# Two pauses in the order of a gated recurrence beside a projection

## The chip, the cores and the metric

One Trainium2 chip, one of its cores. The metric is the device time of one execution in microseconds (us); the kernel before was run three times, with one more execution under the hardware profiler. Engines are named PE (TensorE), DVE (VectorE), ACT (ScalarE), POOL (GpSimd) and SP (SyncE, which here only issues transfers).

## The reference, cut to what matters

The whole program is two transformer layers followed by a third block with another mixer, all in float32, 512 positions, width 1024. The change touches the mixer of the third block alone. It projects the positions `hx` (512 x 1024) and, for some columns, a context `hc` (256 x 1024) with one weight matrix, runs a bidirectional gated recurrence over four heads of 128 (first the context, then the positions), and an attention of 8 heads over positions and context:

```python
px = jnp.split(hx @ w_in[l], IN_SPLIT_IDX, axis=-1)     # q k v | hq hi ff fb hg
pc = jnp.split(hc @ w_in[l], IN_SPLIT_IDX, axis=-1)
...
fg = lb_d + (1.0 - lb_d) * jax.nn.sigmoid(f)            # hgrn2_prep
return silu(q) * HG_HEAD_DIM**-0.5, 1.0 - fg, i, jnp.log(fg)
...
# gla_chunked: S_t = diag(f_t) S_{t-1} + k_t v_t^T, o_t = S_t^T q_t
...
o = rmsnorm(o_f + flip(o_b), gain) * jax.nn.silu(g)     # readout
...
x = x + mx[2] * (jnp.concatenate([att_x, hg_x], axis=-1) @ w_out[l])
```

## The kernel before, in words

**Products.** Every projection streams its weights from memory in chunks of 128 output columns. ACT copies a chunk to a rounded half `w_hi` (`split_high`, line 160), DVE subtracts it to get the rest `w_lo` (`split_low`, line 166), two chunks ahead of their use, and PE makes three matmuls for each 128 rows of the weight (line 196): hi times hi, hi times low, low times hi. The accumulator banks 0 and 1 take turns.

**The second mixer** (`SecondMixer`, from line 1930) has 26 chunks, in the order of `SB_LIST`: the query of heads 0 and 1, then for each head its two gates `ff`, `fb`, (for heads 2 and 3 also `hq`) and its values `i`, and last k, v, four q and four `hg`. A chunk is cut into **parts** of 12 matmuls: two wide ones (512 positions) and, for the gates, values, k and v, two more on the context (256 positions), into bank 2. The 24 chunks behind the first pair make 76 parts, numbered p = 0 to 75. Parts 24 to 37 are head 2's: ff, fb (wide, wide, context, context each), hq (wide, wide), i (wide, wide, context, context); parts 38 to 51 are head 3's in the same way; 52 to 59 are k and v, 60 to 75 q and hg, wide only.

**The recurrence** is cut into 56 **jobs**: a head has two directions (a unit u is one of them), a unit has seven levels. One job n is a chain over four engines: DVE takes two differences of cumulated logs (lines 2295, 2296), ACT their exp (line 2162), POOL two multiplies (lines 2061, 2062), PE the level product (line 2452), and DVE puts the masked result into the weights (`select`, line 2318). Round these lie steps of a unit or a head at fixed job numbers (`due(n, first, every, number)`): on PE turning values (line 2462; n = 0 and 1 of each 14) and decayed keys (line 2469; n = 2 and 3, 9 and 10), the sums (lines 2479, 2482), the output (lines 2501, 2504; n = 18, 32, 46, 60) and its mean (line 2509; n = 20, 34, 48, 62); on ACT the copies of what PE turned (`v_out`, line 2132, n = 4 and 5 of each 14; `kd_out`, line 2124, n = 6 and 7 of each 7), `prepare` (lines 2111 to 2115, n = 1 of each 7), the output's square and copy (lines 2145, 2146; n = 22, 36, 50, 64), its ln and exp (lines 2152, 2154; n = 24, 38, 52, 66); on DVE the four scans of a head (lines 2282, 2284; `SCANS`, before the difference of n = 13, 27, 41), the states (lines 2303 to 2309, n = 3 of each 7, from 10), the gain (line 2336; n = 26, 40, 54, 68). The turned blocks all go through bank 5, so each turning waits until the copy of the turning before it is done.

**What sets the order.** No scheduler: each engine runs one loop over p and does at each p what belongs there. PE does part p, then job `job(p - 14)`. ACT does at p first the copy of the chunk that PE has just ended (`result`, lines 2084, 2087, with the split of the chunk two further on), then the sigmoids of a head if p is in `SIGMOIDS`, the logs if p is in `LOGS`, then job `job(p - 11)`, then steps of the attention's heads (`SQUARES`, `head_mean`). DVE does at p the low half of the split, job `job(p - 11)`, and head gains and ropes (`GAINS`, `TURNS`). POOL runs over the jobs themselves; behind jobs 8, 20 and 34 (`GATES`) it makes the next head's gates and keys (lines 2027 to 2037), and `TURN_AT` puts five rope multiplies (line 2050) behind jobs. Sigmoids wait for the head's gate chunks, gates on POOL for the sigmoids, logs on ACT for the keys from POOL, scans on DVE for the logs. What of the jobs is left when the parts are out runs in the first slots u of the attention's loop (u < `TAIL`): PE job `job(62 + u)`, ACT and DVE `job(65 + u)`, each in front of that slot's attention work. The function between slot and job number is

```python
        PAUSES = ()
        SIGMOIDS = {8: 0, 20: 1, 32: 2, 46: 3}
        LOGS = {11: 0, 22: 1, 34: 2, 48: 3}
...
        def job(q):

            return None if q in PAUSES else q - sum(s < q for s in PAUSES)
```

The attention of 32 units (8 heads by 4 blocks) then runs logits (lines 2585, 2586), exp (2253), scaling, turning (2597, 2601) and values (2613). Its first logits wait for keys and queries that ACT and DVE split behind the last chunk's copy.

Of the kernel before, what the change touches and what calls it, by code (L numbers as in the profile page):

```python
# [78 lines left out]
def build(nc, A, out):  # L79
    with ExitStack() as ctx:  # L80
# [1800 lines left out]
        NT = 6  # L1881
        NR = NT - 1
        U2 = 8 * NB
        TAIL = 10
        AHEAD = 11
        PE_AT = 14
        MEANS = {61: 0, 62: 1, 64: 2, 66: 3, 68: 4, 70: 5}
# [1 line left out]
        SQUARES = {58: (0, 1), 62: (2,), 64: (3,), 66: (4,), 68: (5,)}  # L1889
        GAINS = {61: 0, 64: 1, 66: 2, 68: 3, 70: 4}  # L1890

        PAUSES = ()
        SIGMOIDS = {8: 0, 20: 1, 32: 2, 46: 3}
        LOGS = {11: 0, 22: 1, 34: 2, 48: 3}
        GATES = {8: 1, 20: 2, 34: 3}
        SCANS = {-1: 0, 13: 1, 27: 2, 41: 3}

        def job(q):

            return None if q in PAUSES else q - sum(s < q for s in PAUSES)  # L1900

        TURN_AT = [c - AHEAD + 1 - len(PAUSES) for c in GAINS]

# [84 lines left out]
        class SecondMixer(Stage):  # L1988
# [85 lines left out]
            def scalar(self, act):  # L2074
# [16 lines left out]
                def sigmoid(hd):  # L2091
                    self.there(act, SB_LIST.index(("ff", hd)))
                    self.there(act, SB_LIST.index(("fb", hd)))
                    for u in (2 * hd, 2 * hd + 1):
                        for f in (bx(u), bc(u)):
                            nc.scalar.activation(f, f, ACT.Sigmoid).then_inc(g["sig"], 1)

                def gate_logs(hd):
                    act.wait_ge(g["k"], 4 * hd + 4)
                    for u in (2 * hd, 2 * hd + 1):  # L2100
                        for f in (bx(u), bc(u)):
                            nc.scalar.activation(f, f, ACT.Ln).then_inc(g["ln"], 1)
# [53 lines left out]
                def decays(n):  # L2156
                    if n is None:
                        return
                    if 0 <= n < JOBS:
                        act.wait_ge(g["diff"], n + 1)  # L2160
                        d = dec[:, n % 4, :]
                        nc.scalar.activation(d, d, ACT.Exp).then_inc(g["exp"], 1)  # L2162
                    hd = due(n, 2, 2 * LEVELS, HG)
                    if hd is not None:
                        diag_out(hd)
                    u = due(n, 1, LEVELS, U7)
                    if u is not None:
                        prepare(u)
                    for half in range(2):
                        hd = due(n, 4 + half, 2 * LEVELS, HG)  # L2170
                        if hd is not None:
                            v_out(hd, half)
                        u = due(n, 6 + half, LEVELS, U7)
                        if u is not None:
                            kd_out(u, half)
                    hd = due(n, 22, 2 * LEVELS, HG)
                    if hd is not None:
                        o_out(hd)
                    hd = due(n, 24, 2 * LEVELS, HG)
                    if hd is not None:  # L2180
                        o_rstd(hd)
# [18 lines left out]
                for p in range(len(PARTS)):  # L2200
                    if p in ENDED:
                        result(ENDED[p])
                    if p in SIGMOIDS:
                        sigmoid(SIGMOIDS[p])
                    if p in LOGS:
                        gate_logs(LOGS[p])
                    decays(job(p - AHEAD))
# [33 lines left out]
                for u in range(U2 + HIGH + 1):  # L2241
                    if u < TAIL:
                        decays(job(len(PARTS) - AHEAD + u))
# [23 lines left out]
            def vector(self, dve):  # L2267
# [53 lines left out]
                def gla(n):  # L2321
                    if n is None:
                        return
                    if n in SCANS:
                        sum_gates(SCANS[n])
                    if 0 <= n < JOBS:
                        difference(n)
                    u = due(n, 10, LEVELS, U7)
                    if u is not None:
                        states(u)  # L2330
                    if 3 <= n < JOBS + 3:
                        select(n - 3)
                    hd = due(n, 26, 2 * LEVELS, HG)
                    if hd is not None:
                        dve.wait_ge(g["rstd"], 2 * hd + 2)
                        nc.vector.scalar_tensor_tensor(hq(hd), hq(hd), gain_hg[:, :], ors, ALU.mult, ALU.mult).then_inc(g["y"], 1)
# [57 lines left out]
                for u in range(U2 + HIGH + 2):  # L2394
                    v = u - 2
                    if u < TAIL:
                        gla(job(len(PARTS) - AHEAD + u))
# [31 lines left out]
            def tensor(self, pe):  # L2429
# [81 lines left out]
                def gla(n):  # L2511
                    if n is None:
                        return
                    if 0 <= n < JOBS:
                        level(n)
                        u, l = n // LEVELS, n % LEVELS
                        if l < 2 and u % 2 == 0:
                            turn_values(u // 2, l)
                        if l in (2, 3):
                            turn_keys(u, l - 2)  # L2520
                        if l == 5:
                            sums(u)
                    hd = due(n, 18, 2 * LEVELS, HG)
                    if hd is not None:
                        output(hd)
                    hd = due(n, 20, 2 * LEVELS, HG)
                    if hd is not None:
                        mean(hd)
                    hd = due(n, -2, 2 * LEVELS, HG)
                    if hd is not None:  # L2530
                        diagonal(hd)
# [85 lines left out]
                for u in range(U2 + HIGH):  # L2617
                    if u < TAIL:
                        gla(job(len(PARTS) - PE_AT + u))
# [169 lines left out]
```

## Time and profile before

| | us |
|---|---|
| runs of the kernel before | 2244.57, 2246.85, 2250.64 (median 2246.85) |
| profiled execution | 2245.27 |
| its span, first to last instruction | 2243.6, granted clock 0.971 |
| PE busy | 2090.5 (93%) |
| DVE busy | 1245.8 (56%) |
| ACT busy | 900.9 (40%) |
| POOL busy | 323.5 (14%) |
| second mixer: parts, about | 1380 to 1690 of the span |
| its attention, about | 1694 to 1809 of the span |

Times in the views are microseconds from the start of the span. A row of the timeline gives the start, the duration, the engine, the line, the operation, out<-in, and in brackets how long the engine was idle before it and which engine and line released it; matmuls overlap, so their distance is read from their starts. The granted clock is a share of full speed, 2.4 GHz; its other level is 1.2 GHz. Level n is the job's group of eight matmuls of line 2452: level 14 starts at 1470.33, level 24 at 1510.52.

### The profile page before, as it was taken

Reading aid. Unit: us, or ns where it says so; the run is one execution under the profiler, and the core shown is the slowest. Engines: PE = TensorE matmul, PEld = TensorE weight load, DVE = VectorE, ACT = ScalarE, POOL = GpSimd, SP = SyncE. Lnnn points to the kernel's source line nnn. Section 1 sums busy time; section 2 is a strip of 40 time slices with the busy share of each in tenths; the row PEclk is TensorE's granted clock in tenths of the full one; section 3 lists DMA queues with packets and bytes.
Section 4 is the critical chain, followed back from the end, with each engine's and each line's share of the span. In section 5 each row is a group of like instructions: output and inputs, shape, how many; then the busy total and the mean of one; then the engine's idle time right before and its main releaser. Section 6 shows DMA issues by size and latency. Waiting matters only on the chain. (4 is left out here: it accounts for less than half of the span.)

```text
span 2243.6 us, 27319 instructions
## 1 busy us (share of the span) xinstructions
PE 2090.5 (93%) x9710; PEld 1656.2 (74%) x9710; DVE 1245.8 (56%) x1922; ACT 900.9 (40%) x1394; POOL 323.5 (14%) x404
## 2 busy tenths in 40 slices
PE   8999889999999899999999988799887898999997
PEld 6666547888888677778888866688765676888885
DVE  3666437788767746766564353666646534333333
ACT  4433543444422444344443234566447624322222
POOL 0033311100000201010000013666420002000000
PEclk9999899999999999999999998899998999999998
DMA  5211002566544222223333211110110022233321
GB/s 185 76 56 38 1 20 75 169 192 192 160 154 164 98 90 85 85 66 93 95 101 116 91 56 56 39 37 31 57 48 1 1 75 76 93 93 100 115 91 49
DMA packets 52628, 191.84 MB, mean 86 GB/s; under 512 B 5792, under 2 KB 8512, under 8 KB 52288
## 3 DMA queue, kind: packets, MB, share of 16 engines
q1 hardware_dynamic: 44672, 163.07, 22.8%
q0 software_dynamic: 7344, 27.27, 3.9%
q8 instruction: 50, 0.82, 0.2%
q10 hardware_dynamic: 528, 0.40, 0.1%
q14 instruction: 34, 0.28, 0.0%
HBM read 187.05 MB, written 3.67 MB: 85 GB/s over the span
## 5 line engine op out<-in xcount | busy, mean ns | idle before, releaser
L196 PE MATMUL psum<-xH,w_hi 128*128 128x512 f32 x1800 | 731.5, 406 | 38.4 <-DVE xL L1305 22.9
L196 PE MATMUL psum<-xL,w_hi 128*128 128x512 f32 x1800 | 712.6, 396 | 0.0
L196 PE MATMUL psum<-xH,w_lo 128*128 128x512 f32 x1800 | 712.0, 396 | 0.0
L166 DVE TENSOR_TENSOR w_lo<-w_raw,w_hi 128x1024 fp32r<-128x1024 f32 (+1 forms) x273 | 357.8, 1311 | 361.1 <-ACT w_hi L160 360.9
L160 ACT ACTIVATE w_hi<-w_raw 128x1024 fp32r<-128x1024 f32 (+1 forms) x273 | 303.4, 1111 | 396.1 <-PE psum L196 393.8
L196 PEld LDWEIGHTS psum<-xH,w_hi 128*128 128x128 f32 x1800 | 345.4, 192 | 139.8 <-DVE xL L1305 37.7
L196 PEld LDWEIGHTS psum<-xH,w_lo 128*128 128x128 f32 x1800 | 344.7, 191 | 74.2
L196 PEld LDWEIGHTS psum<-xL,w_hi 128*128 128x128 f32 x1800 | 345.6, 192 | 71.6 <-issue 3.4
L196 PE MATMUL psum<-hidH,w_hi 128*128 128x512 f32 x528 | 206.2, 391 | 0.0
L196 PE MATMUL psum<-hidH,w_lo 128*128 128x512 f32 x528 | 205.4, 389 | 0.0
L196 PE MATMUL psum<-hidL,w_hi 128*128 128x512 f32 x528 | 205.4, 389 | 0.0
L1380 DVE SCALAR_TENSOR_TENSOR gate_value<-psum,cols,gate_value 128x511 f32<-128x511 f32 x88 | 66.0, 750 | 134.4 <-ACT gate_value L1353 133.4
L1353 ACT ACTIVATE gate_value<-psum,cols 128x512 f32<-128x512 f32 x88 | 60.7, 689 | 164.9 <-PE psum L196 164.9
L1316 POOL TENSOR_SCALAR xT<-y,cols 128x512 f32<-128x512 f32 x32 | 40.1, 1262 | 553.5 <-DVE y L1297 553.5
L196 PEld LDWEIGHTS psum<-hidL,w_hi 128*128 128x128 f32 x528 | 99.1, 188 | 21.1 <-issue 0.5
L196 PEld LDWEIGHTS psum<-hidH,w_hi 128*128 128x128 f32 x528 | 99.1, 188 | 21.0 <-issue 0.5
L196 PEld LDWEIGHTS psum<-hidH,w_lo 128*128 128x128 f32 x528 | 99.1, 188 | 20.6
L2318 DVE COPY_PREDICATED gla_weights<-gla_masks,psum 128x512 f32<-128x512 uint8 x56 | 41.3, 738 | 76.1 <-PE psum L2452 74.4
L2162 ACT ACTIVATE sb_hT<-sb_hT 128x512 f32<-128x512 f32 x56 | 34.8, 628 | 112.5 <-DVE sb_hT L2296 112.4
L612 ACT ACTIVATE logits<-logits,stat 128x128 f32<-128x128 f32 (+3 forms) x64 | 36.0, 562 | 107.9 <-DVE stat L742 107.8
L742 DVE CUSTOM_DVE_ANT_0 logits<-psum,addend 128x128 f32<-128x128 f32 (+3 forms) x64 | 31.4, 491 | 82.6 <-PE psum L850 80.1
L1383 DVE SCALAR_TENSOR_TENSOR gate_value<-psum,cols,gate_value 128x510 f32<-128x510 f32 x88 | 65.9, 749 | 11.1 <-DVE gate_value L1380 2.8
(312 smaller groups left out, 2541.9 us busy)
## 6 DMA issues: line engine op xcount, KB each, us to landing
w_raw<-in_up SPq DMA_DIRECT2D x132, 512.0 KB, 3.5
w_raw<-in_down SPq DMA_DIRECT2D x48, 704.0 KB, 4.1
mod_raw<-in_mod POOLq DMA_DIRECT2D x48, 512.0 KB, 3.8
w_raw<-in_sb_in SPq DMA_DIRECT2D x26, 512.0 KB, 3.5
w_raw<-in_ev_in SPq DMA_DIRECT2D x23, 512.0 KB, 3.5
w_raw<-in_od_in SPq DMA_DIRECT2D x20, 512.0 KB, 3.5
w_raw<-in_ev_out SPq DMA_DIRECT2D x8, 512.0 KB, 3.5
w_raw<-in_od_out SPq DMA_DIRECT2D x8, 512.0 KB, 3.5
```

What stands on the lines that cost most here:

```text
L160: nc.scalar.activation(w_hi[:, s % SPLIT, 0:w.cols], raw[:, s, 0:w.cols], ACT.Copy).then_inc(w.high, 1)
L166: nc.vector.tensor_tensor(w_lo[:, s % SPLIT, 0:w.cols], raw[:, s, 0:w.cols], w_hi[:, s % SPLIT, 0:w.cols].bitcast(F32), ALU.subtract).then ...
L196: mm = nc.tensor.matmul(acc, a[:, slot % SPLIT, cut], b[:, k0 + k, :], start=start and n == 0, stop=stop and n == 2)
L612: nc.scalar.activation(t, t, ACT.Exp, bias=stat[:, 0, s:s + 1], scale=-1.0, accum_out=stat[:, 1, s:s + 1]).then_inc(a["exp"], 1)
L742: nc.vector.tensor_tensor_reduce(out=tl[:, s % RING, 0:n], in0=logits_bank(s)[:, 0:n], in1=Xa[:, s % 3, 0:n], scale=-1.0 if kind == "a" el ...
L1316: nc.gpsimd.tensor_scalar(dst, yt[:, t % 3, 0:self.n], self.gain(t), self.shift(t), ALU.mult, ALU.add)\
L1353: nc.scalar.activation(value if j % 2 else gate, bank[j % 2][:, :], ACT.Copy, scale=self.tap(i, j, 2)).then_inc(ff["tap"], 1)
L1380: nc.vector.scalar_tensor_tensor(y[:, 1:T], acc[:, 0:T - 1], self.tap(i, j, 1), y[:, 1:T], ALU.mult, ALU.add).then_inc(ff["conv"], 1)
L1383: self.emptied(nc.vector.scalar_tensor_tensor(y[:, 2:T], acc[:, 0:T - 2], self.tap(i, j, 0), y[:, 2:T], ALU.mult, ALU.add), j)
L2162: nc.scalar.activation(d, d, ACT.Exp).then_inc(g["exp"], 1)
L2318: nc.vector.copy_predicated(aT[:, hd % 2, :, :], level_mask[d][:, l * P:(l + 1) * P].unsqueeze(1).to_broadcast([P, NB, P]), bank[3 + n % 2 ...
```

## The change

It puts two slots, q = 14 and 15, without a job between job 13 and job 14, so that from job 14 on every engine meets job n two parts later (PE at p = n + 16, ACT and DVE at n + 13). The logs of heads 1, 2 and 3 go one slot later. The sigmoids, chunk copies and head steps keep their parts. The jobs run in the attention's loop up to its slot 11 instead of 9; `TURN_AT` follows the pauses by itself (49, 52, 54, 56, 58 instead of 51, 54, 56, 58, 60).

```diff
-        TAIL = 10
+        TAIL = 12
         AHEAD = 11
         PE_AT = 14
...
-        PAUSES = ()
+        PAUSES = (14, 15)
         SIGMOIDS = {8: 0, 20: 1, 32: 2, 46: 3}
-        LOGS = {11: 0, 22: 1, 34: 2, 48: 3}
+        LOGS = {11: 0, 23: 1, 35: 2, 49: 3}
         GATES = {8: 1, 20: 2, 34: 3}
         SCANS = {-1: 0, 13: 1, 27: 2, 41: 3}
...
         TURN_AT = [c - AHEAD + 1 - len(PAUSES) for c in GAINS]
```

## Rows read from the trace of the kernel before

**Rows 1.** Windows: window, its length, busy of PE, PEld, DVE, ACT, POOL, granted clock, DMA
```profile
1470.00:1512.00 42.00, 39.19 (x261) 35.05 (x259) 28.55 (x46) 28.95 (x46) 28.46 (x33) 1.00 0.12 38
1512.00:1522.00 10.00, 5.03 (x20) 4.22 (x21) 5.06 (x9) 1.96 (x4) 2.05 (x2) 0.83 0.16 54
```

**Rows 2.** Waits of PE, 1466 to 1694: us in total, times, longest
```profile
PE psum L2469 <- ACT gla_kd_tm L2124: 14.7, 6, 5.4
PE psum L2462 <- ACT gla_v_tm L2132: 4.7, 3, 1.6
...
PE psum L2547 <- ACT sb_hT L2189: 2.1, 1, 2.1
PE psum L2564 <- DVE values L2371: 1.3, 1, 1.3
```

**Rows 3.** Timeline of PE: levels, and a turning of values that waits
```profile
1466.67 1.06 PE L2452 MATMUL psum<-gla_mixed 128*128 128x128 f32 x8
1470.33 1.05 PE L2452 MATMUL psum<-gla_mixed 128*128 128x128 f32 x8
...
1477.06 0.41 PE L2462 MATMUL psum<-ident,sb_hc 128*128 128x128 f32 x2 [1.57 <-ACT gla_v_tm L2132]
...
1565.63 1.05 PE L2452 MATMUL psum<-gla_mixed 128*128 128x128 f32 x8
1567.96 1.06 PE L2452 MATMUL psum<-gla_mixed 128*128 128x128 f32 x8
```

**Rows 4.** Timeline of PE: the wait behind level 24
```profile
1516.97 0.66 PE L2469 MATMUL psum<-ident,gla_keys_decayed 128*128 128x128 f32 x2 [5.39 <-ACT gla_kd_tm L2124]
1517.28 0.78 PE L196 MATMUL psum<-xH,w_hi 128*128 128x512 f32 x1
...
1519.99 0.44 PE L196 MATMUL psum<-xH,w_hi 128*128 128x512 f32 x1
...
1521.19 0.39 PE L196 MATMUL psum<-xH,w_lo 128*128 128x512 f32 x1
```

**Rows 5.** Timeline of DVE in front of that wait
```profile
1507.71 0.74 DVE L2318 COPY_PREDICATED gla_weights<-gla_masks,psum 128x512 f32<-128x512 uint8 x1
1508.34 0.74 DVE L2336 SCALAR_TENSOR_TENSOR sb_hT<-sb_hT,gla_gain,sb_hc 128x512 f32<-128x512 f32 x1
1510.20 1.51 DVE L166 TENSOR_TENSOR w_lo<-w_raw,w_hi 128x1024 fp32r<-128x1024 f32 x1 [1.11 <-ACT w_hi L160]
1511.63 1.21 DVE L2282 TENSOR_TENSOR_SCAN sb_hT<-gla_inside,sb_hT 128x512 f32<-128x512 f32 x1
```

**Rows 6.** Timeline of ACT at p = 32, from the chunk's copies to a copy of turned keys
```profile
1483.00 0.38 ACT L2084 ACTIVATE sb_hc<-psum 128x256 f32<-128x256 f32 x1
...
1484.83 1.28 ACT L2096 ACT_TABLE_LOAD   x1
1486.12 0.63 ACT L2096 ACTIVATE sb_hT<-sb_hT 128x512 f32<-128x512 f32 x1
...
1489.74 0.36 ACT L2124 ACTIVATE gla_kd_tm<-psum 128x256 f32<-128x256 f32 x1
```

**Rows 7.** Timeline of POOL: first and last of the eight gate and key steps
```profile
1487.99 1.30 POOL L2027 TENSOR_SCALAR sb_hT<-sb_hT,gla_lb 128x512 f32<-128x512 f32 x1 [3.53 <-ACT sb_hc L2096]
...
1492.65 0.40 POOL L2033 TENSOR_SCALAR gla_kc<-sb_hc 128x256 f32<-128x256 f32 x1
```

**Rows 8.** Timeline of DVE: first and last of the states of the last unit
```profile
1666.70 0.28 DVE L2303 COPY gla_state<-psum 128x128 f32<-128x128 f32 x1
...
1668.17 0.69 DVE L2309 TENSOR_TENSOR gla_since<-sb_hT,gla_since 128x512 f32<-128x512 f32 x1
```

**Rows 9.** Timeline of PE: output of the last head begins; first logits
```profile
1684.93 0.38 PE L2501 MATMUL psum<-gla_weights,gla_v_tm 128*128 128x128 f32 x2
...
1694.57 0.55 PE L2585 MATMUL psum<-keys_split,queries_split 128*128 128x256 f32 x1 [3.21 <-DVE queries_split L2385]
```

**Rows 10.** Timeline of ACT: square of the last head's output
```profile
1687.80 0.60 ACT L2145 ACTIVATE sb_hc<-psum 128x512 f32<-128x512 f32 x1 [2.23 <-PE psum L2504]
```

## The prediction, made before the changed kernel was run

> **What bounds it now.** I read the page's engine totals first (TensorE is the busiest by far), then busy time and granted clock by stretch: between the long waits of the second mixer TensorE is busy 39.2 of 42 us at clock 1.00, and around one of them 5.0 of 10 us at 0.83 [rows 1]. So this stage is bound by TensorE plus its waits, and a stretch of other engines' work counts only where TensorE waits for it. Then TensorE's waits [rows 2] and, for each kind, the instructions around it on all engines. I call p the part number and n the job; before, TensorE runs job n behind part n + 14 and ScalarE/VectorE run it at slot n + 11. With the two pauses every job from 14 on moves two parts later on all engines, while the copies of finished columns, the weight splits, sigmoids and head work keep their part. The change adds and removes no arithmetic; it shifts two interleaved sequences against each other.
>
> Lengths used: a wide part with its level takes 3.66 us (1466.67 to 1470.33), one with the 256 context columns 2.33 us (1565.63 to 1567.96) [rows 3].
>
> **Step 1, the scan wait.** Before, VectorE at p = 38 splits a weight (L166), then runs the four scans, then the difference of job 27, and ScalarE's copy of the turned keys (L2124) lies behind that job's exp. TensorE, done with job 24, waits 5.39 us [rows 4]. The six matmuls behind it take 2.71 us (1517.28 to 1519.99), the next five 1.20 (to 1521.19) [rows 4]: the first at the 1.2 GHz level, the others at 2.4 GHz, and the granted clock of the stretch is 0.83 [rows 1]. That is 1.3 us more. The same happens at job 38. Afterwards the scans come at p = 40, no longer behind a split. From VectorE's select of job 23 at 1507.71 the scans could follow after the gain multiply, at 1509.1 instead of 1511.6 [rows 5]: 2.5 us sooner. But part 40 is a context part where part 38 was a wide one, so TensorE arrives 1.33 us sooner too (3.66 - 2.33). Gain 1.2 us if VectorE runs undisturbed; GpSimd would now be at its multiplies beside the scans, and how far that slows VectorE no row of this place shows, so I take 0.5 us a wait, bounds 0 and 1.2. Twice: **-1.0**.
>
> **Step 2, the short waits.** Turning values waits three times, 4.7 us in all [rows 2], each behind VectorE's split, difference, state chain (2.1 us [rows 8]), select, difference and then ScalarE's exp and copy (1477.06, wait 1.57 [rows 3]). Afterwards jobs 28 and 29 stand behind context parts 44 and 45: the split is gone from the chain, but TensorE comes sooner. Counting from the end of level 27: select 0.7, difference 0.7, states 2.1, select 0.7, difference 0.7, exp 0.6, copy 0.6 = 6.7 with gaps, against 2.33 + 2.33 + 0.35 = 5.0 for TensorE: wait 1.8. In head 1 the two pauses leave VectorE two wide parts, so 0.8. Sum 0.8 + 1.8 + 1.8 = 4.4 instead of 4.7: **-0.3**, bounds -3 (no wait in any) and +2. The waits at jobs 17, 31 and 45 (the six of L2469 less two of 5.39 and one at the end of 1.44: 14.7 - 10.8 - 1.44 = 2.4 us [rows 2]) fall: the part between the two turns becomes a wide one, 1.33 us longer than the wait of 0.8. **-2.4**.
>
> **Step 3, the new wait.** This is what speaks against the change. SIGMOIDS stays at 32 and 46. Before, the sigmoids run in front of job 21's (35's) exp, and what is queued behind them is a copy that TensorE needs three parts later. Afterwards they run in front of job 19's (33's), with the value copy of line 2132 behind, and TensorE needs that copy in the very slot: turning the keys of job 16 (30), behind part 32 (46), waits for it. ScalarE's chain is context copy, column copy, weight split, table load, four sigmoids, table load, exp, copy: 1483.00 to 1490.10, 7.1 us [rows 6]. It starts when ScalarE has delivered the value copy of step 2, which by that step is late, about when TensorE resumes; TensorE then has 0.4 of turns, 2.85 of part and 0.8 of level, 4.0 us. New wait 3.1 us, plus the 1.3 us of slow matmuls: 4.4, twice: **+8.8**. Bounds: 1.7 us without clock loss if ScalarE is free when the context part ends (twice 1.7 = 3.4), and twice 6.7, a full wait as today's long one [rows 4] = 13.4.
>
> Each switch of function costs ScalarE one load of 1.28 us with the next instruction 0.01 us behind [rows 6]; the chain holds two. The Trainium skill, page "ScalarE: Activation LUTs", section "What ACT_TABLE_LOAD costs", gives 1283 ns for the load and a drain of 1380 ns on top for every switch. By that the chain would be 2.8 us longer and step 3 would cost 5.5 us more, an estimate from the page; this trace shows no such drain, so I give it no chance of its own.
>
> **Step 4, the logs.** LOGS goes one slot later in heads 1 to 3 while jobs go two, so the four logs now stand in front of job 22 (36) rather than 23 (37), and in front of its output copy. They wait for GpSimd's gates, 1487.99 to 1493.05, 5.1 us [rows 7], which start behind the multiply of job 20, and that follows level 17. Counted from the end of level 18: gates done at 3.0 (multiply 1.5 + 5.1 - one wide part with level 3.66), logs 2.1, load 1.3, exp 0.6, keys of the next unit 2.2, square and copy 1.1 = 10.3; TensorE reaches its mean after output 2.6, 3.66, sums 0.9 and 2.33 = 9.5: about **+0.7** twice = **+1.4**, bounds 0 and +5. In head 1 (22 to 23, ahead of the pauses) ScalarE runs job 11's exp first and finishes its logs about 1 us later, but VectorE's scans then fall behind GpSimd's multiplies instead of beside them: **0**, bounds -0.5 and +1, the 1 us if that cover is gone.
>
> **Step 5, the end of the projection.** The states of the last unit (VectorE, 2.1 us, 1666.70 to 1668.86 [rows 8]) move from p = 70 to 72, in front of the copy that TensorE waits for (L2564, 1.3 us before [rows 2]). TensorE brings 0.8 of level 55 more, so the wait grows by 1.3. The wait of 2.1 us for a head mean's copy behind two table loads (L2547 [rows 2]) moves from part 63 to 65, behind one more rope step: +0.5. The head waits on VectorE keep about their sum, and one of them is partly filled by a mean. **+1.9**, bounds 0 and +4.
>
> **Step 6, attention.** Output 3 (24 operations, from 1684.93 until ScalarE's square starts at 1687.80, less 0.3 that the next part overlaps [rows 9, 10]) leaves the parts and goes ahead of the first logits, where TensorE idles 3.2 us behind its mean [rows 9]: **-2.6**, the gap being its cover. Its square (0.6 us [rows 10]) and the copy like it, 1.1 us overlapped, now stand in front of the second softmax exp, and the Ln/Exp pair with its loads in front of the fourth instead of the second; the pipeline had idle slots there: **+0.5**, bounds -1 and +3. The queues of SP and GpSimd keep their order, and no DMA moves; TAIL = 12 only admits slots that the last job step (68, now at u = 5) does not reach.
>
> **Sum**: -1.0 - 0.3 - 2.4 + 8.8 + 1.4 + 0 + 1.9 - 2.6 + 0.5 = +6.3 us. The profiled execution took 2245.27 us (span 2243.6), 1.6 below the median 2246.85. It would become 2251.6; the median 2253.2, +0.28%.
>
> **Rivals.**
> - *The new wait is mostly absorbed* (step 3 at its low end, 3.4 instead of 8.8): VectorE and ScalarE are ahead after two parts without a job, the value copy comes in time. For it: ScalarE is busy 29 of 42 us between the long waits [rows 1]. Against: after the pauses the sequences lock again level by level. Sum about +1: 2248. Chance 0.20.
> - *Slower still*: VectorE's operations double beside GpSimd's, the value copy comes 1 to 2 us later, step 3 gives its full 13.4 us and step 4 another 2. Sum about +13: 2260. It decides from the point where the wait in front of turning the keys of jobs 16 and 30 passes 4.5 us. Chance 0.20.
> - *Faster*: the scans, freed from the split, give the whole 1.2 us each, the value waits vanish (-3 or more), and step 3 stays at 1.7 us. -2.4 - 3 - 2.4 + 3.4 + 0 + 0.5 - 2.6 + 0 = -6.5: 2240. For it: it needs only that VectorE is never disturbed. Against: the states chain stands before the value copy in all heads. It decides from the point where turning the keys of job 16 waits under 2 us. Chance 0.08.
> - *It doesn't do what it says*: the pauses hold for every engine through the one function job, and GpSimd counts jobs, so I see no way; 0.02, at no change.
> - My forecast: 0.50.
>
> **How the numbers follow.** A measurement of this kernel tells about 0.3%, 6.7 us, from no change. My forecast of +6.3 has a spread of some 4 us and lies at that edge: of its 0.50 I give 0.27 to slower and 0.23 to the same. Same: 0.23 + 0.18 + 0.02 = 0.43 (0.02 of the first rival falls above). Slower: 0.27 + 0.20 + 0.02 = 0.49. Faster: 0.08. The range reaches from the low end of the forecast and most of the first rival, 2245, to most of the second, 2262; about 0.2 is left out.
>
> **What would show it.** TensorE's wait on L2469 for ACT L2132 (there is none before), two of about 3 us, in front of the keys of jobs 16 and 30, each followed by some six matmuls at the lower clock level; the two waits of 5.4 at 4.3 to 5.4; the waits of 0.8 gone; L2564's wait at 2.6; outputs of head 3 in front of the first logits with less idle there. The forecast is wrong if no such wait on L2132 stands there, or if the time moves by what another stage does.

## The result, and the profile after

The changed kernel took 2261.45 us (median of four runs, 2260.12 to 2261.71) against 2246.55 for the kernel before (four runs, 2244.57 to 2250.64): a ratio of 1.0061, 95% interval 1.0049 to 1.0073. By the medians it is 14.9 us slower, by the ratio 13.7, where +6.3 was forecast. The profiled execution took 2261.24 us, its span is 2259.6 at a granted clock of 0.968.

**Where the time lies.** I cut the third block's mixer at three events that every kernel here has: ScalarE's first copy of a finished chunk (line 2087), the first logits on TensorE (line 2585) and the end of the last value product (line 2613). The first comes from the view of one line, here of the changed kernel (engine, operation, output and input, count, shortest, median and longest ns, first and last start):

```profile
L2087 ACT ACTIVATE sb_hT<-psum x26: 574/596/601, 1367.8 to 1702.6; 128x512 f32<-128x512 f32 x26
```

Before, the three are 1366.1, 1694.57 [rows 9] and 1807.53; after, 1367.8, 1706.60 and 1823.93. So the projection went from 328.5 to 338.8 us (+10.3), the attention from 113.0 to 117.3 (+4.4); the stage itself starts 1.7 us later, which is not the change's. The two stretches as windows, the same columns as rows 1, of the kernel before (projection from the end of its wait at job 10 on, then attention) and the changed one:

```profile
1455.60:1694.50 238.90, 208.59 (x1248) 179.22 (x1248) 142.37 (x217) 125.95 (x213) 109.40 (x121) 0.97 0.13 40
1694.57:1807.53 112.96, 95.98 (x512) 67.39 (x512) 65.29 (x119) 73.08 (x136) 0.00 (x0) 0.94 0.00 1
```
```profile
1457.50:1706.60 249.10, 212.80 (x1246) 184.14 (x1247) 135.66 (x217) 127.30 (x213) 107.39 (x121) 0.95 0.12 39
1706.60:1823.93 117.33, 97.83 (x514) 68.00 (x514) 65.09 (x119) 74.07 (x138) 0.00 (x0) 0.94 0.00 1
```

Of the 10.2 us by which the projection's window grew, TensorE is busy 4.2 longer for the same products, and 6.0 longer idle; the granted clock (the last column but two) falls from 0.97 to 0.95.

**The waits**, the view of [rows 2] for the changed kernel, from 1466 to the first logits:

```profile
PE psum L2469 <- ACT gla_kd_tm L2124: 11.6, 3, 5.1
PE psum L2469 <- ACT gla_v_tm L2132: 5.9, 2, 2.9
PE psum L2462 <- ACT gla_v_tm L2132: 5.7, 3, 2.2
PE psum L2542 <- DVE head_sin L2348: 3.7, 3, 1.9
PE psum L2547 <- ACT sb_hT L2189: 3.0, 1, 3.0
PE psum L2564 <- DVE values L2371: 2.5, 1, 2.5
PE psum L2509 <- ACT sb_hT L2146: 2.3, 2, 1.2
PE psum L2585 <- DVE queries_split L2385: 1.4, 1, 1.4
```

(In each line: us in total, times, longest.) The second line is the wait that step 3 had forecast, and the kernel before has none of its kind [rows 2]. TensorE around the first of its two places, in front of the keys of job 16:

```profile
1481.58 0.41 PE L2462 MATMUL psum<-ident,sb_hc 128*128 128x128 f32 x2 [1.43 <-ACT gla_v_tm L2132]
1481.74 0.48 PE L196 MATMUL psum<-xH,w_hi 128*128 128x512 f32 x1
...
1484.58 1.05 PE L2452 MATMUL psum<-gla_mixed 128*128 128x128 f32 x8
1488.58 0.87 PE L2469 MATMUL psum<-ident,gla_keys_decayed 128*128 128x128 f32 x3 [2.94 <-ACT gla_v_tm L2132]
1489.10 0.78 PE L196 MATMUL psum<-xH,w_hi 128*128 128x512 f32 x1
...
1494.37 1.12 PE L2452 MATMUL psum<-gla_mixed 128*128 128x128 f32 x8
```

and ScalarE's chain that it waits for, which answers to [rows 6]:

```profile
1480.86 0.58 ACT L2132 ACTIVATE gla_v_tm<-psum 128x512 f32<-128x512 f32 x1
1481.34 0.38 ACT L2084 ACTIVATE sb_hc<-psum 128x256 f32<-128x256 f32 x1
...
1483.16 1.28 ACT L2096 ACT_TABLE_LOAD   x1
1484.46 0.63 ACT L2096 ACTIVATE sb_hT<-sb_hT 128x512 f32<-128x512 f32 x1
...
1486.24 1.28 ACT L2162 ACT_TABLE_LOAD   x1
1487.53 0.63 ACT L2162 ACTIVATE sb_hT<-sb_hT 128x512 f32<-128x512 f32 x1
1488.07 0.37 ACT L2132 ACTIVATE gla_v_tm<-psum 128x256 f32<-128x256 f32 x1
```

Read them together: the first value copy ends a wait of 1.43 us, and right behind it in ScalarE's queue stand the chunk's copies, the split and four sigmoids, 1481.34 to 1488.44, the 7.1 us of the forecast; TensorE has 4.1 us of work (1481.58 to the end of the level at 1485.64). Then the part behind the wait: its twelve matmuls start within 2.84 us where the clock is full (1481.74 to 1484.58) and within 5.27 us here (1489.10 to 1494.37). All twelve run at the 1.2 GHz level, where six did in [rows 4]. At the second of the two places, in front of the keys of job 30, only the first five do, and the part takes 3.91 us. The Trainium skill, page "ScalarE: Activation LUTs", section "What ACT_TABLE_LOAD costs", would add a drain of 1380 ns to each of the two loads; the rows have the next activation 0.01 to 0.02 us behind each load, as in [rows 6], so the trace doesn't agree.

A third part is slow too, and no step of the forecast has it. In front of the turned values of job 43 TensorE waits 2.16 us; the part behind it takes 4.42 us instead of 2.84, with its third to ninth matmul at the low level. Behind the same wait of 2.16 us at job 29 (until 1549.50) the part takes 2.85.

```profile
1616.85 0.41 PE L2462 MATMUL psum<-ident,sb_hc 128*128 128x128 f32 x2 [2.16 <-ACT gla_v_tm L2132]
1617.02 0.48 PE L196 MATMUL psum<-xH,w_hi 128*128 128x512 f32 x1
...
1621.44 1.05 PE L2452 MATMUL psum<-gla_mixed 128*128 128x128 f32 x8
```

**The attention** of the changed kernel on TensorE, from the first logits (units 0 and 1) on:

```profile
1706.60 0.36 PE L2585 MATMUL psum<-keys_split,queries_split 128*128 128x256 f32 x1 [1.40 <-DVE queries_split L2385]
...
1714.35 2.07 PE L2509 MATMUL psum<-sb_hc,mean_of 128*128 128x512 f32 x2 [6.10 <-ACT sb_hT L2146]
1715.44 1.20 PE L2585 MATMUL psum<-keys_split,queries_split 128*128 128x256 f32 x1
```

and on ScalarE:

```profile
1712.33 0.90 ACT L2253 ACTIVATE probs<-psum,stat 128x768 f32<-128x768 f32 x1
...
1713.22 0.59 ACT L2145 ACTIVATE sb_hc<-psum 128x512 f32<-128x512 f32 x1
1713.70 0.60 ACT L2146 ACTIVATE sb_hT<-psum 128x512 f32<-128x512 f32 x1
1714.18 0.91 ACT L2253 ACTIVATE probs<-psum,stat 128x768 f32<-128x768 f32 x1
...
1718.73 0.90 ACT L2253 ACTIVATE probs<-psum,stat 128x768 f32<-128x768 f32 x1 [3.55 <-DVE stat L2403]
```

The square and copy of head 3's output stand in front of the second exponential. TensorE's mean (line 2509), which waits for both (the row names the copy, line 2146, the later of the two), stands in front of the second logits, which here and below are those of unit 2, the first that need a bank freed by an exponential. So they start at 1715.44, 2.2 us after the end of the exponential that frees their bank (1713.23), at the low clock level, and ScalarE idles 3.55 us in front of the third exponential, where the pipeline should fill.

### The profile page after: what moved, and what is told of

Read it like the earlier page. It is cut to its first block and busy times, and to the rows that moved or that the text cites. A ratio compares the mean times of both kernels' runs of the same rounds, so it can differ in the third digit from the quotient of the medians.

```text
span 2259.6 us, 27321 instructions
## 1 busy us (share of the span) xinstructions
PE 2099.0 (93%) x9710; PEld 1662.5 (74%) x9710; DVE 1239.3 (55%) x1922; ACT 902.9 (40%) x1396; POOL 320.7 (14%) x404
## 5 line engine op out<-in xcount | busy, mean ns | idle before, releaser
L196 PEld LDWEIGHTS psum<-xL,w_hi 128*128 128x128 f32 x1800 | 345.5, 192 | 70.7 <-issue 2.6
```

The lines of the kernel that those rows point to most:

```text
L196: mm = nc.tensor.matmul(acc, a[:, slot % SPLIT, cut], b[:, k0 + k, :], start=start and n == 0, stop=stop and n == 2)
```

## The experiments

One table holds them all. "Before" is the kernel before, timed beside them: 2247.03 for the first four experiments, 2245.61 for the next three, 2245.91 for the last three; the changed kernel's ratio is against the 2246.55 above. Projection and attention are cut as above, from the one profiled execution of each kernel, and their change against the kernel before (328.5 and 113.0) stands in brackets. Executions of one kernel differ by up to 9 us among themselves, and a profiled one lies up to 3.3 us off its median (2249.97 against 2253.26 for the kernel with the sigmoids following), so a difference of 1 or 2 us between two of these cuts alone shows little.

| kernel | median us | ratio to before, 95% | projection | attention |
|---|---|---|---|---|
| changed | 2261.45 | 1.0061, 1.0049–1.0073 | 338.8 (+10.3) | 117.3 (+4.4) |
| e1_logs_only | 2249.29 | 1.0010, 1.0001–1.0020 | 332.1 (+3.6) | 113.0 (0) |
| e2_pauses_only | 2265.01 | 1.0075, 1.0057–1.0093 | 345.5 (+17.0) | 117.4 (+4.4) |
| e3_sigmoids_follow | 2253.26 | 1.0029, 1.0019–1.0038 | 331.6 (+3.1) | 117.4 (+4.4) |
| e4_tail_only | 2249.71 | 1.0015, 1.0005–1.0025 | 325.9 (-2.6) | 118.6 (+5.6) |
| e5_mean_later | 2242.89 | 0.9993, 0.9982–1.0004 | 325.8 (-2.7) | 113.2 (+0.2) |
| e6_scans_split | 2238.32 | 0.9963, 0.9948–0.9978 | 320.4 (-8.1) | 114.5 (+1.5) |
| e7_change_scans_split | 2253.66 | 1.0035, 1.0020–1.0050 | 335.7 (+7.2) | 117.2 (+4.2) |
| e8_split_and_tail | 2235.78 | 0.9955, 0.9942–0.9969 | 317.7 (-10.8) | 114.6 (+1.6) |
| e9_change_mean_later | 2259.34 | 1.0058, 1.0042–1.0073 | 339.0 (+10.5) | 115.9 (+2.9) |
| e10_change_mended | 2248.59 | 1.0012, 1.0002–1.0021 | 325.4 (-3.1) | 115.8 (+2.8) |

My theory from the traces: the pauses move jobs against the chunk work of the other engines, and three collisions pay for it: ScalarE's sigmoids in front of the value copy, the logs in front of the output's square, and the mean in the attention. The rival: jobs behind two empty slots are late as such, wherever the other work stands.

**One part of the change alone: the logs, in the kernel before.**

```diff
-        LOGS = {11: 0, 22: 1, 34: 2, 48: 3}
+        LOGS = {11: 0, 23: 1, 35: 2, 49: 3}
```

> The kernel before with the new LOGS alone (23, 35, 49), no pauses. The logs are off TensorE's path in every head, so theory A (the time is lost where jobs and parts are shifted against each other) expects no change: within 1.5 us of the kernel before, the two waits of 5.4 us behind levels 24 and 38 within 0.3 us, and no wait of L2469 on L2132. The rival, that the later logs are what delays the output's square and copy, expects the waits of L2509 on L2146 (1.2 us each, twice) here too and +3 to +5 us.

The time rose by 2.3 us, and the two waits that I had expected to stay (within 0.3 us) grew from 5.39 to 6.71. The waits that the rival expected, of line 2509 for line 2146, don't come. VectorE in front of the first of them, and GpSimd beside it:

```profile
1510.34 1.23 DVE L166 TENSOR_TENSOR w_lo<-w_raw,w_hi 128x1024 fp32r<-128x1024 f32 x1 [1.99 <-ACT w_hi L160]
1511.49 1.86 DVE L2282 TENSOR_TENSOR_SCAN sb_hT<-gla_inside,sb_hT 128x512 f32<-128x512 f32 x1
```
```profile
1510.41 1.85 POOL L2062 TENSOR_TENSOR gla_mixed<-gla_k,sb_hT 128x256 f32<-128x256 f32 x1
```

This kernel's stage starts 0.9 us earlier (1365.2), so against the stage VectorE gets the split 1.04 us later than in [rows 5], because ScalarE's logs and then its ln and exp with their loads now stand later; the split itself is 0.28 shorter, and the first scan takes 1.86 instead of 1.21 us while GpSimd's multiply runs beside it. 1.04 - 0.28 + 0.65 = 1.4 us, which is what the wait and the earlier start of the stage give (1517.46 against 1516.97, plus 0.9). The Trainium skill, page "GPSIMD Engine Reference", section "1. Specifications", has the two engines share their interfaces to the memory when a VectorE instruction has two inputs there; the trace agrees with it for this scan.

**The other part alone: the pauses with the old logs, that is the changed kernel with that line put back.**

> The changed kernel with the old LOGS (22, 34, 48): the pauses alone. The sigmoids still stand in front of the value copy, so theory A expects the two waits of L2469 on L2132 at 2.9 us unchanged. The logs now stand one job earlier against GpSimd's gates, in front of the copy of turned keys at job 21 (35), so ScalarE holds for the gates longer: 0 to +3 us against the changed kernel (2261 to 2264), with a wait of L2479 or L2509 of 1 to 2 us. The rival, that LOGS made the loss, expects it below 2253.

2265.01 us, 1 above the most expected: with the pauses in, the logs a slot later are worth some 3 us, though the two intervals overlap. The waits say what they avoid, 1466 to the first logits:

```profile
PE psum L2469 <- ACT gla_kd_tm L2124: 15.0, 3, 6.8
...
PE psum L2479 <- ACT gla_kd_tm L2124: 4.2, 2, 2.1
```

A new wait of 2.1 us twice in front of the sums (line 2479), and scan waits of 6.8 instead of 5.1. The first wait on the value copy stays at 2.93, as expected; the second is 1.36 us instead of 2.93, a miss. The copy comes as late as in the changed kernel, 7.0 us behind the turning of job 29, but here TensorE's part in between runs mostly at the low level and takes 4.42 instead of 2.85 us: slow matmuls that stand in front of a wait are taken out of it. So the change's line for the logs mends the pauses in part, and is no source of its loss.

**The suspected collision removed: the sigmoids and logs of heads 2 and 3 move with the jobs.** From the changed kernel:

```diff
-        SIGMOIDS = {8: 0, 20: 1, 32: 2, 46: 3}
-        LOGS = {11: 0, 23: 1, 35: 2, 49: 3}
+        SIGMOIDS = {8: 0, 20: 1, 34: 2, 48: 3}
+        LOGS = {11: 0, 23: 1, 36: 2, 50: 3}
```

> The changed kernel with SIGMOIDS at 34 and 48 and LOGS at 36 and 50, two parts later like the jobs. Theory A expects both waits of L2469 on L2132 (2.9 us each) and their slow matmuls gone (2.5 and 1.1 us of longer parts) and both waits of L2509 on L2146 (1.2 us each) gone: 8 to 12 us less than the changed kernel, 2250 to 2253. What is left over the kernel before, +4 to +6 us, is then attention and the end of the projection. The rival, that two parts without a job in front of them cost by themselves (later jobs, later everything), expects less than 3 us back.

8.2 us under the changed kernel (the ratios give 7.2), and the projection is 7.2 us shorter. ScalarE at the place where the sigmoids stood, and TensorE's waits from 1466 to the first logits:

```profile
1475.50 0.58 ACT L2132 ACTIVATE gla_v_tm<-psum 128x512 f32<-128x512 f32 x1
...
1480.29 0.37 ACT L2132 ACTIVATE gla_v_tm<-psum 128x256 f32<-128x256 f32 x1
```
```profile
PE psum L2469 <- ACT gla_kd_tm L2124: 14.4, 3, 6.8
PE psum L2462 <- ACT gla_v_tm L2132: 5.8, 3, 2.2
...
PE psum L2469 <- ACT gla_v_tm L2132: 0.5, 1, 0.5
```

The second value copy comes 4.8 us behind the first instead of 7.2, the waits on it fall from 5.9 to 0.5, and the mean's two (line 2509, 2.3) are gone. Part of that is paid back at the scans, 6.16 and 6.77 us where it was 5.06 and 5.09; in front of the second, the scans begin 1.1 us later behind TensorE's level than in the changed kernel, and the context scan (line 2284) takes 1.25 instead of 0.66 us with a multiply beside it; the first scan takes 1.85 us here and 1.86 there. The edit moves the logs too, so it removes two of the three collisions at once, the sigmoids' (+9.4 us, waits and slow parts, by the forecast's way of counting) and the logs' (+2.3). Together they are shown, by their removal, to be most of the projection's loss (7.2 of 10.3 net, with 2.8 us given back at the scans); the rival would have left it. The attention's loss is untouched.

**The attention's part alone: the kernel before with the two empty slots at 60 and 61**, so that only jobs from 60 on move (the five rope multiplies of `TURN_AT` keep their jobs):

```diff
-        TAIL = 10
+        TAIL = 12
-        PAUSES = ()
+        PAUSES = (60, 61)
-        TURN_AT = [c - AHEAD + 1 - len(PAUSES) for c in GAINS]
+        TURN_AT = [c - AHEAD + 1 for c in GAINS]
```

> The kernel before with the pauses at slots 60 and 61 instead of 14 and 15: only the last head's output, mean, square, ln/exp and gain move into the attention as in the change; everything of jobs 0 to 59 stays. The trace of the changed kernel shows 4.4 us more from the first logits to the end of the attention and 2.6 less in front of them: theory A expects +1.8 us (bounds 0 and +4), with a wait of about 6 us of L2509 on L2146 behind the second logits. The rival, that what moved into the attention is hidden there as my prediction had it (+0.5), expects -2 us.

The time rose by 2.7 us (the ratio gives 3.4), where +1.8 was expected. The projection gains 2.6 us and the attention loses 5.6, with the same wait of 6.11 us for the mean. The forecast's -2.6 of step 6 is there, and the loss behind it belongs to the steps of the jobs from 60 on alone: output, mean, square and copy, ln and exp, gain.

**The same with the mean of head 3 one turn later,** behind the second logits:

```diff
-                    hd = due(n, 20, 2 * LEVELS, HG)
+                    hd = due(n, 20, 2 * LEVELS, HG) if n < 62 else HG - 1 if n == 63 else None
```

> The tail of the change alone, with TensorE's mean of head 3 one turn later: behind the second logits of the attention, not in front of them. If the 6.1 us that the mean waited for ScalarE's square in the attention is what cost the tail its time, the wait of the mean goes, the second logits wait some 4 us for their exponentials only, and the time is some 2 us under that of the tail alone (2249.7), about 2247.7, level with the kernel before. Rival: the third logits then meet the same late chain (the square and copy on ScalarE stand in front of its exponentials either way), the waits of the first eight parts sum to what they did, and the time stays at 2249.7 or above.

The attention is back at 113.2 us, 5.4 less, and the time falls by 4.9 by the ratios, more than the 2 expected; against the kernel before the median is 2.7 us lower, but the interval holds 1. TensorE's waits from the first logits on, the two tail kernels:

```profile
PE psum L2509 <- ACT sb_hT L2146: 6.1, 1, 6.1
...
PE psum L2585 <- ACT probs L2253: 4.3, 3, 3.2
PE psum L2597 <- ACT probs_t L2230: 2.8, 3, 1.9
```
```profile
PE psum L2585 <- ACT probs L2253: 7.1, 2, 5.1
...
PE psum L2597 <- ACT probs_t L2230: 2.9, 3, 1.9
```

13.2 us of waits in these rows become 10.0: the second logits wait 5.1 us, and not for a mean that waits 6.1 and then runs slowly, and the logits of unit 5 wait 2.0 instead of 3.2. The rest of the 5.4 is TensorE busy 2.1 us longer on the same work, at a granted clock of 0.93 against 0.95. Over all traces the step is smaller: with the mean in front of the second logits the attention takes 117.2 to 118.6 us (five kernels, 117.6 on average), with the mean behind them 113.2 to 115.9 (four, 114.9), and with nothing moved into it 113.0 to 114.5 (three, 113.5). The mean's place is worth some 2.7 us, and what else moved some 1.4.

**The two scan waits, which are in both kernels.** The kernel before, with the scans of a head's two units issued apart:

```diff
-        SCANS = {-1: 0, 13: 1, 27: 2, 41: 3}
+        SCANS = {-1: 0, 7: 1, 12: 2, 21: 3, 26: 4, 35: 5, 40: 6, 49: 7}
...
-                def sum_gates(hd):
-                    dve.wait_ge(g["ln"], 4 * hd + 4)
+                def sum_gates(unit):
+                    dve.wait_ge(g["ln"], 2 * unit + 2)
...
-                    for u in (2 * hd, 2 * hd + 1):
+                    for u in (unit,):
```

> The kernel before, with VectorE's two scans of a head issued one by one: the first where the pair was or a job earlier, the second some eight jobs later; nothing else changed. If TensorE's waits of 4.6 to 5.4 us behind level 24 and its twins come from the pair of scans, gate sums and decays standing in one block ahead of two states on VectorE, the wait behind job 10 goes, those behind levels 24 and 38 fall from 5.39 to about 2 us each, the matmuls behind them run at the full clock again (2.99 instead of 4.3 us), and the time is 8 to 15 us under the kernel before: 2232 to 2239. Rival: VectorE lags by the sum of its work over the whole stretch and the block only says where the lag shows; then the waits move to the second scans and their sum stays, and the time is within 3 us of 2247.

7.3 us under before, just short of the 8 expected. The wait at job 10 fell from 4.57 to 0.48, while an earlier one for GpSimd's multiply (line 2452) grew from 3.53 to 5.12. Those behind levels 24 and 38 fell only from 5.39 to 4.1, and slow matmuls still follow, six at once behind the first and seven, from the fifth on, behind the second:

```profile
1510.61 0.66 PE L2469 MATMUL psum<-ident,gla_keys_decayed 128*128 128x128 f32 x2 [4.10 <-ACT gla_kd_tm L2124]
1510.92 0.78 PE L196 MATMUL psum<-xH,w_hi 128*128 128x512 f32 x1
...
1570.70 0.41 PE L2469 MATMUL psum<-ident,gla_keys_decayed 128*128 128x128 f32 x2 [4.05 <-ACT gla_kd_tm L2124]
...
1571.94 0.63 PE L196 MATMUL psum<-xL,w_hi 128*128 128x512 f32 x1
```

So the block of four scans is one cause of those waits, and not the whole.

**The same split in the changed kernel.**

> The changed kernel with the same split of the scans. The waits for scans and those for the sigmoid's chain are then apart: the first theory has 8 to 15 us less than the changed kernel (2261.4), so 2246 to 2253, with the two waits of 2.9 us for the value copies and that of 6.1 us in the attention still there. If they are one thing (VectorE late, whatever the cause), the waits for the value copies shrink too and the time is near that of the other split kernel, within 5 us. If the split moves the lag only, it stays at 2258 or above.

7.8 us under the changed kernel (the ratios give 5.8), just short of the 8 expected, with the two waits of 2.9 for the value copies and the 6.1 in the attention unchanged. So these are costs apart from the scans'. The logs' is not: the scan waits fell from 5.06 and 5.09 to 3.58 and 2.30, but the mean's two waits (line 2509) grew from 1.16 and 1.18 to 2.42 and 2.41, which gives 2.5 us of it back.

**Both edits that gained, in the kernel before: the split scans and the tail with the later mean.**

> The kernel before with both edits that gained by themselves: the scans issued one by one (8 us under before by itself) and the tail's two jobs in the attention with the mean behind the second logits (2 us under before by itself). They lie in different stretches, the one before level 39, the other behind the first key part without a job, so the gains should add: 9 to 11 us under the kernel before, about 2236. Rival: with less waiting in the projection the late chain of the last head meets other work and one gain eats the other; then the time is that of the split alone (a ratio of 0.996) or above.

2235.78 us, 10.1 under before (ratio 0.9955): they add. It is the fastest of these kernels, 26 us under the changed one. Its two empty slots are at 60 and 61, behind the last sigmoids, logs and scans.

**The later mean in the changed kernel.**

> The changed kernel with the mean of head 3 one turn later, as in the tail experiment, where the same edit took 5 us. If the changed kernel's loss in the attention is that mean in front of the second logits, it loses 4 to 6 us here too: 2255.5 to 2257.5, with the wait of 6.1 us gone and the projection's waits as they were. Rival: in the changed kernel the last units are bound by VectorE behind the exponentials, whatever TensorE's order: then less than 2 us, above 2259.5.

A miss: the time is 2.1 us lower by the medians and 0.7 by the ratios, not 4 to 6; the attention is 1.5 us shorter, not 5.4, and the ratio, 1.0058, is inside the interval of the changed kernel's. The wait of 6.1 is gone (5.14 for the second logits, to the hundredth that of the tail kernel with the same edit), yet the attention takes 2.7 us more than that kernel's. The section on the hardware has where.

**All of it in the changed kernel: sigmoids and logs following, scans split, mean later.**

> The changed kernel with all that the runs so far showed: sigmoids and logs of the later heads with the pauses (8 us by itself), scans one by one (6 to 8 us), the mean of head 3 a turn later (4 to 6 us). If each named wait is a cost of its own, about 2240 to 2244, that is 4 to 8 us under before, but 4 us or so above the same two edits without the pauses (about 2236): the two pauses gain nothing themselves. Rival: the pauses are worth something once their waits are gone; then this is the fastest, under 2234.

2248.59 us, at least 4.6 above what was expected: 12.9 us under the changed kernel, and still not faster than before. Its scan waits are 5.26 and 5.70, where the same split had left 4.1 without the pauses, two parts of 2.84 us behind waits of 2.16 take 4.4, and its attention is at 115.8. The pauses at 14 and 15 gain nothing that these runs could find: the best kernel without them is 12.8 us faster than the best with them. No other place for the logs and scans under these pauses was tried.

## Why the prediction was right or wrong

The time, 2261.45, lies 0.5 us inside the upper end of the stated range, and the way was right: slower. The size was not, +14.9 for +6.3. That the range reached so far is owed to the case "slower still", whose mechanism didn't come, so the hit is in part luck. Of the prediction's two signs of being wrong, the first stayed away (the two waits on line 2132 are there), and the second came in part: 4.4 us were lost in another stage, the attention. By its own steps, each against the measured size:

- *Step 1, scan wait, -1.0:* the waits went from 5.39 and 5.39 to 5.06 and 5.09, -0.6, and slow matmuls stayed (the context part behind each takes 2.7 us, 1.5 elsewhere). Right in kind, and so is the disturbance that no row could size: the first of the two long scans takes 1.86 us beside a GpSimd multiply in both places, 1.21 in [rows 5].
- *Step 2, short waits:* the three of jobs 17, 31 and 45 are gone, -2.4 as forecast. The values wait 5.7 instead of 4.7, +1.0 where -0.3 was forecast: 1.43, 2.16 and 2.16 against 0.8, 1.8 and 1.8. The slow part behind the last of them, 1.6 us, is in no step. (6.7 less 5.0 is 1.7, not 1.8; the sums of steps 4 and 5 are off by 0.1 in the same way, which changes nothing.)
- *Step 3, the new wait, +8.8:* the place and the chain were right, 2.94 and 2.93 us where 3.1 was forecast. The clock's term was mis-sized: 1.3 us a time was taken from [rows 4], and it measured 2.4 (5.27 - 2.84) and 1.1 us. Together +9.4; removing its cause, and the logs' wait with it, took 7.2 us net from the projection.
- *Step 4, logs, +1.4:* two waits of 1.16 and 1.18 us in front of the mean, +2.3. For head 1 "0" held (the wait at job 10 is 4.73 instead of 4.57). What the forecast didn't see is that the logs also set when the scans come; it shows in the kernel with the logs alone, where the line costs 2.3 us.
- *Step 5, end of the projection, +1.9:* L2564 waits 2.5 (2.6 forecast), L2547 3.0 (+0.9 instead of +0.5), the head waits on VectorE 0.7 less: +1.4.
- *Step 6:* the output moved into the idle time in front of the first logits, -2.6, as forecast and as the tail alone shows (projection -2.6); of that, 1.8 is the wait in front of the first logits, 3.21 before and 1.40 after. The attention, forecast at +0.5, measured +4.4. This is the step that failed. "The pipeline had idle slots there" looked at ScalarE's time, not at the order on TensorE: the mean waits 6.10 us for the square and copy and stands in front of the second logits, so the logits wait for it. The forecast put a price on what moved to ScalarE and none on what moved to TensorE with it. The wait is shown, its price less sharply: moving the mean took 5.4 us from the attention in the tail kernel and 1.5 in the changed one, some 2.7 over all traces. The rest of the +4.4 goes with the square and copy in front of the second exponential and with the clock; which of them has how much stays open.

The sum of the measured projection steps is -0.6 + 1.0 - 2.4 + 9.4 + 2.3 + 1.4 - 2.6 = +8.5 of +10.3. The slow part at job 43 has 1.6 of the other 1.8; 0.2 isn't assigned. With the attention's +4.4 that is +14.7 by the cuts and +14.9 by the medians. The forecast's projection steps summed to +5.8 and its attention to +0.5. So of what it was short by, the attention has 3.9 us, the projection's steps 2.7 and the rest 1.8, nearly all of it the slow part that no step has. The case "slower still" came nearest in its total, 2260, but not by its mechanism: the wait on the value copies never passed 3 us.

## What to carry to other kernels

When interleaved sequences are shifted against each other, list for every engine what stands in front of each hand-over at the new place, and include the engine that receives. A step costs nothing by its length if it fits an idle slot, and much by its place if it waits for something and work that could run is queued behind it. Work that belongs to the sequence (here sigmoids and logs) has to move with it. Shifting only the tail, with its mean behind the ready logits, gave 2.7 us, at the edge of what the runs can tell, where shifting most of the sequence lost 14.9. A block of independent work in front of a hand-over, such as a pair of scans of which one is needed, is worth splitting first.

## What the runs showed of the hardware

- **The price of a wait in TensorE's clock isn't fixed by the wait.** All figures are for the part of twelve matmuls behind it, which takes 2.84 us at the full clock. Behind the two waits of 2.94 and 2.93 us of the changed kernel it took 5.27 and 3.91, and in the kernel with the split scans on top 4.43 and 5.27, with the same work on both sides; behind waits of 2.16 us it took 2.85 or about 4.4; behind 5.39 us 4.15, and behind the two of 6.71 us with the logs alone 5.08 and 4.05. So for an estimate a wait near 3 us or longer costs 1 to 2.5 us of clock besides itself, and one of 2.2 us nothing or 1.6. The slow matmuls needn't be the first ones: in the fence of the split scans above they begin with the fifth. What sets it isn't known from these runs. The attention shows it too. Windows of the tail kernel with the later mean, and of the changed kernel with it, each from its first logits on:

```profile
1689.80:1710.90 21.10, 12.02 (x42) 8.46 (x43) 13.93 (x24) 18.87 (x28) 0.00 (x0) 0.76 0.00 0
1710.90:1720.90 10.00, 9.99 (x58) 7.31 (x59) 5.17 (x10) 5.97 (x13) 0.00 (x0) 1.00 0.00 0
```
```profile
1705.70:1726.80 21.10, 10.55 (x43) 7.08 (x43) 13.92 (x24) 18.86 (x28) 0.00 (x0) 0.81 0.00 0
1726.80:1736.80 10.00, 10.00 (x45) 7.51 (x46) 3.01 (x6) 3.91 (x8) 0.00 (x0) 0.72 0.00 0
```

  The order is the same, and the three long waits end at the same distance from the first logits (6.77, 15.31 and 21.07 us in one, 6.77, 15.32 and 21.08 in the other). The second is 1.99 us long in one and 3.20 in the other, because the clock rose again sooner there (0.81 against 0.76) and TensorE was done earlier, so in these 21.1 us the clock costs nothing. In the next 10, TensorE is busy throughout in both, at 1.00 in one (58 matmuls) and 0.72 in the other (45). That goes with the 2.7 us by which the two attentions differ. One execution of each is profiled, so this may be a difference of the executions and not of the kernels: the four of the changed kernel with the later mean lie between 2256.29 and 2262.46 us at clocks of 0.967 to 0.970, and the profiled one took 2261.11.
- **VectorE's scan and a GpSimd multiply lengthen each other, the later one as a rule.** A scan of 512 positions takes 1.19 to 1.22 us alone, and 1.74 to 1.88 when a multiply runs as it begins (1.86 in the kernel with the logs alone, 1.85 in the one with the sigmoids following). Where the scan began first, it kept its 1.21 us and the multiply took 1.54 instead of 0.73: 1512.75 and 1512.94 in the changed kernel with the split scans, 1508.40 and 1508.59 in the one with all edits. Two that began within 0.01 us of each other went the same way (split scans on the kernel before, 1561.01: scan 1.21, multiply 1.74). What runs beside what depends on ScalarE's order, so moving ScalarE's logs changed VectorE's speed.
